# The last output group added onto x in its PSUM banks, and the last merged block turned later

## The chip, the core and the metric

The kernel runs on one core of a Trainium2 chip. The metric is the device time of one execution in microseconds; the profile's span runs from the first to the last instruction. The engines are TensorE (PE, with its weight loads PEld), VectorE (DVE), ScalarE (ACT), GpSimd (POOL) and SyncE (SP), which issues most of the DMAs.

## The reference

One decoder block over 256 tokens of width 2048: two token mixers, joined by sigmoid gates, an output projection, a residual and a final norm.

```python
xn = rmsnorm(x, norm_w)
rq, rk, rv, rz, dq, dk, dv, dz, g_ret, g_diff = split(xn @ w_in)
o_ret = rmsnorm(retention(rq, rk, rv)) * silu(rz)
o_diff = rmsnorm(diff_attention(dq, dk, dv, lam), subln_w) * (1 - lam_init) * silu(dz)
mixed = sigmoid(g_ret) * (o_ret @ w_ret_up) + sigmoid(g_diff) * (o_diff @ w_diff_up)
h = x + mixed @ w_out
out = rmsnorm(h, final_norm_w)
```

The change touches the last three lines: how the last quarter of `mixed` is laid out for the projection, the projection with `w_out`, the residual and the norm.

## The kernel before

**Units.** Every weight is read once, in units of 512 KB: 384 units in a row, through a ring of four buffers (`raw`, `w_hi`, `w_lo`). A unit is loaded by SyncE, rounded to `w_hi` by ScalarE (L711), its rest put into `w_lo` by VectorE (L1038), and multiplied by TensorE in three passes (hi by hi, hi by lo, lo by hi). The left side is split in the same way. ScalarE and VectorE split a unit three units ahead of TensorE (`AHEAD`), as soon as the unit four before it is done. The load of unit n waits on SyncE until unit n-4 is split. Every engine's queue is in order, and the Python loops fix what stands behind what: on SyncE a loop over n, on ScalarE and VectorE a loop over steps s, each of which first splits unit s+3 and then does its other work.

**The last two phases.** From `U_TAIL` on (units 320 to 351) `o_diff @ w_diff_up` is made in four groups j of 512 columns, eight units each. When a group is done, `merge_diff` multiplies it by the gate, `add_diff` adds it to `mixed`, `turn_mixed` transposes 32x32 squares into `squares_t` on VectorE, SyncE's `turn_mixed` moves the squares to their place in `rot` by 2 x 4 DMAs (L510), and `read_mt_hi` and `read_mt_lo` (L912, L1364) split the turned block into four k-tiles of `xt_hi` and `xt_lo`. From `U_OUT` on (units 352 to 383) `mixed @ w_out` is made in two groups of 1024 columns, 16 k-tiles each; tile k of the first is unit 352+k. TensorE holds `own` and `shared` banks, four each, and the two groups swap them. Tiles 4 and 5, and 10 and 11 (`SEVEN_AT`), are multiplied as a 2x2 block product in seven instead of eight products. That needs sums of token tiles (`sum_tokens`, split by `round_token_sums` and `rest_of_token_sums`) and sums of weight blocks (`sum_weights` L970 to L976, which stands in front of the split of the unit before them and waits until both units have landed; `round_sums` and `rest_of_sums` L990 split the sums). The seven products go to the own banks and, as parts, to the shared ones.

**The block and the group.** The last block (j = 3) gives k-tiles 12 to 15. It is merged in step 32, added and transposed in step 34, turned by SyncE in front of the load of unit 362 (tile 10), and read in step 38. TensorE waits for it (`ready`, count 8) in front of tile 12. x is loaded again for each block into `gate`, behind the loads of tiles 4 and 12 for the last two.

**The end of a group.** `copy_first` (ScalarE) and `join_shared` (VectorE, four instructions, L1019 to L1024) turn the parts into one summand for each of the four output tiles. `add_x` (L1374) adds x to them, `add_own` (L1382) adds the own bank. In the second group the last four tiles are multiplied bank by bank, 12 matmuls each, so that the banks end one after another. Row 0 is squared, normed and stored while row 1 is still being made. For row 1 the last tile is squared in two halves, on ScalarE (L923) and on VectorE (L1439), then come the sums (L1431), POOL's power (L662), and the scaling of the last two tiles on VectorE (L1446) and of the first two on ScalarE (L932).

## Time and profile before

| | |
|---|---|
| median of 3 runs | 1096.87 us (1094.86 to 1097.81) |
| the profiled execution | 1095.23 us |
| its span | 1093.4 us |
| TensorE busy | 1077.5 us, 99% |
| VectorE busy | 746.3 us, 68% |
| ScalarE busy | 540.5 us, 49% |
| mean granted TensorE clock | 0.995 |
| start of the first output group, last matmul | 992.3 us, 1083.2 us |

The engines overlap, so their busy times do not add up to the span. A matmul row shows 0.39 us of which about 0.23 us is its own turn, as the next starts then. The granted clock is a share of 2.4 GHz.

### The profile page before, as it was taken

What the parts mean: (1) busy time and instruction counts of PE and PEld (TensorE: products, weight loads), DVE (VectorE), ACT (ScalarE), POOL (GpSimd) and SP (SyncE); (2) the same over time, 40 slices, a digit from 0 to 9 for tenths busy, and PEclk for the clock granted to TensorE, in tenths of its full rate; (3) what the DMA queues carried; (4) which work ended last, traced back from release to release, by engine and by line L of the source; (5) the groups of instructions that cost most, each with busy time, mean ns of one, the idle gap of its engine ahead of it and who ended that gap; (6) DMA issues with size and microseconds to landing.
All of it is one profiled execution on the core that took longest, in us unless ns stands there. A gap on an engine that the chain in (4) does not pass through costs nothing.

```text
span 1093.4 us, 13197 instructions
## 1 busy us (share of the span) xinstructions
PE 1077.5 (99%) x4864; PEld 895.5 (82%) x4864; DVE 746.3 (68%) x919; ACT 540.5 (49%) x695; POOL 36.6 (3%) x57
## 2 busy tenths in 40 slices
PE   9999999999999999999999999999999999999996
PEld 7888888888888888888888888888888888887784
DVE  6685574585566688766856676676757674768796
ACT  6654455344555545444654465346544644445453
POOL 0100000000000000000100010000100020000000
PEclk9999999999999999999999999999999999999998
DMA  9887667776666565777576757676767667676653
GB/s 329 301 247 222 175 199 205 202 202 210 195 189 201 186 213 167 222 214 215 177 212 186 239 169 212 191 227 187 200 210 207 187 207 254 225 228 210 230 174 115
DMA packets 133985, 227.98 MB, mean 208 GB/s; under 512 B 14496, under 2 KB 40864, under 8 KB 133408
## 3 DMA queue, kind: packets, MB, share of 16 engines
q1 hardware_dynamic: 133632, 226.86, 67.9%
q8 instruction: 38, 0.62, 0.2%
q10 hardware_dynamic: 288, 0.27, 0.1%
q14 instruction: 27, 0.22, 0.1%
HBM read 210.84 MB, written 2.10 MB: 195 GB/s over the span
## 4 chain that ended last, share of the span: by engine, by line
PE 95%; DVE 2%; DMA 1%; ACT 1%; issue 1%; SPq 0%; DVEq 0%; POOLq 0%; POOL 0%; ACTq 0%
PE bank L1531 26%; PE bank L1529 26%; PE bank L1530 26%; PE bank L1536 4%; PE bank L1537 4%; PE bank L1538 4%; DMA raw<-w_out_dram 1%; PE bank L1599 1%; PE bank L1598 1%; PE bank L1597 1%; DVE w_lo L1038 1%; DMA raw<-w_in_dram 0%; PE bank L1712 0%; PE bank L1501 0%; ACT w_hi L711 0%
## 5 line engine op out<-in xcount | busy, mean ns | idle before, releaser
L1038 DVE TENSOR_TENSOR w_lo<-raw,w_hi 128x1024 fp32r<-128x1024 f32 x364 | 449.2, 1240 | 303.5 <-ACT w_hi L711 302.9
L711 ACT ACTIVATE w_hi<-raw 128x1024 fp32r<-128x1024 f32 x364 | 385.4, 1060 | 473.7 <-PE bank L1531 398.9
L1529 PE MATMUL bank<-w_hi,xt_hi 128*128 128x512 f32 x1136 | 443.3, 390 | 0.0
L1531 PE MATMUL bank<-w_hi,xt_lo 128*128 128x512 f32 x1136 | 442.1, 389 | 0.0
L1530 PE MATMUL bank<-w_lo,xt_hi 128*128 128x512 f32 x1136 | 442.0, 389 | 0.0
L1531 PEld LDWEIGHTS bank<-w_hi,xt_lo 128*128 128x128 f32 x1136 | 213.2, 188 | 44.5
L1530 PEld LDWEIGHTS bank<-w_lo,xt_hi 128*128 128x128 f32 x1136 | 213.3, 188 | 43.8
L1529 PEld LDWEIGHTS bank<-w_hi,xt_hi 128*128 128x128 f32 x1136 | 213.3, 188 | 43.8
L1529 PE MATMUL bank<-w_hi,ot_hi 128*128 128x512 f32 x128 | 49.8, 389 | 0.0
L1530 PE MATMUL bank<-w_lo,ot_hi 128*128 128x512 f32 x128 | 49.8, 389 | 0.0
L1531 PE MATMUL bank<-w_hi,ot_lo 128*128 128x512 f32 x128 | 49.8, 389 | 0.0
L1536 PE MATMUL bank<-w_hi,xt_hi 128*128 128x512 f32 x104 | 41.4, 399 | 3.6 <-DVE w_lo L1038 3.6
L1537 PE MATMUL bank<-w_lo,xt_hi 128*128 128x512 f32 x104 | 41.1, 396 | 0.0
L1538 PE MATMUL bank<-w_hi,xt_lo 128*128 128x512 f32 x104 | 41.0, 394 | 0.0
L1536 PE MATMUL bank<-w_hi,ot_hi 128*128 128x512 f32 x104 | 40.5, 389 | 0.0
L1537 PE MATMUL bank<-w_lo,ot_hi 128*128 128x512 f32 x104 | 40.5, 389 | 0.0
L1538 PE MATMUL bank<-w_hi,ot_lo 128*128 128x512 f32 x104 | 40.5, 389 | 0.0
L655 POOL TENSOR_TENSOR zs<-zs,sub 128x512 f32<-128x512 f32 x8 | 14.1, 1786 | 496.1 <-DVE zs L1105 496.1
L1530 PEld LDWEIGHTS bank<-w_lo,ot_hi 128*128 128x128 f32 x128 | 24.0, 188 | 5.0
L1531 PEld LDWEIGHTS bank<-w_hi,ot_lo 128*128 128x128 f32 x128 | 24.0, 188 | 5.0
L1529 PEld LDWEIGHTS bank<-w_hi,ot_hi 128*128 128x128 f32 x128 | 24.0, 188 | 4.9
L679 ACT ACTIVATE w_hi<-raw 128x1536 fp32r<-128x1536 f32 x8 | 11.9, 1491 | 31.8 <-PE bank L1538 24.7
(182 smaller groups left out, 851.8 us busy)
## 6 DMA issues: line engine op xcount, KB each, us to landing
raw<-w_in_dram SPq DMA_DIRECT2D x284, 512.0 KB, 4.3
raw<-w_ret_up_dram SPq DMA_DIRECT2D x32, 512.0 KB, 4.5
raw<-w_diff_up_dram SPq DMA_DIRECT2D x32, 512.0 KB, 4.8
raw<-w_out_dram SPq DMA_DIRECT2D x32, 512.0 KB, 4.6
rot<-squares_t SPq DMA_DIRECT2D x96, 64.0 KB, 2.4
zs<-squares_t SPq DMA_DIRECT2D x48, 64.0 KB, 2.2
normed<-squares_t SPq DMA_DIRECT2D x48, 64.0 KB, 2.2
raw<-w_in_dram SPq DMA_DIRECT2D x8, 256.0 KB, 4.8
```

Source lines behind the costliest of these rows:

```text
L655: pool.tensor_tensor(z, z, sub08[:, :].unsqueeze(1).broadcast_to([P, 2, V]), ALU.mult) \
L679: act.activation(hi_blocks[:, KU * s + 1:KU * s + 4, :], raw_blocks[:, KU * s + 1:KU * s + 4, :], ACT.Copy) \
L711: act.activation(w_hi[:, s, :, :], raw[:, s, :, :], ACT.Copy).then_inc(hi_ready, 1)
L1038: dve.tensor_tensor(w_lo[:, s, :, :], raw[:, s, :, :], w_hi[:, s, :, :].bitcast(F32), ALU.subtract) \
L1529: pe.matmul(bank[bk][:, :], hi, w_hi[:, s, kk, :], start=k == 0, stop=False)
L1530: pe.matmul(bank[bk][:, :], hi, w_lo[:, s, kk, :], start=False, stop=False)
L1531: return pe.matmul(bank[bk][:, :], lo, w_hi[:, s, kk, :], start=False, stop=k == KT - 1)
L1536: pe.matmul(dst, hi, w_hi_block, start=start, stop=False)
L1537: pe.matmul(dst, hi, w_lo_block, start=False, stop=False)
L1538: return pe.matmul(dst, lo, w_hi_block, start=False, stop=stop)
L1597: pe.matmul(dst, hi, v_hi[:, b, cols], start=start, stop=False)
L1598: pe.matmul(dst, hi, v_lo[:, b, cols], start=False, stop=False)
```

## The change

Five things change.

1. The last block is added in step 36, transposed in step 37, turned by SyncE in front of the load of unit 366 (tile 14) and read in step 41 (`tail_step`). The other blocks keep their places.
2. `sum_tokens` and the two functions behind it work on one pair of tiles at a time; for the output projection the first pair is summed in step 22, the second in step 29 (`TAIL_SUMS`). TensorE waits for each pair by itself.
3. The x loads of the last two blocks go behind the loads of tiles 17 and 18 (`X_AGAIN_AT`). `x_to_banks` copies x from `gate` into the four own banks of the second group, and TensorE's first products of this group add to it. `add_x` falls away for this group. The joined parts are added to the row-0 tiles in `add_own`, and to the row-1 tiles inside their banks (`part_to_bank`); TensorE waits for these before the last products of bank 2 and bank 3.
4. The row-1 tiles of the second group are squared by ScalarE (`square_last`) and scaled by VectorE (`scale_last`) straight from their banks; the halves and one scalar step go.
5. For the second pair of the second group the weight sums are split in front of the split of tile 12, not behind it (`sums_first`).

```diff
+TAIL_SUMS = (2 * UNITS + 6, 3 * UNITS + 5)
+X_AGAIN_AT = (U_TAIL + 20, U_TAIL + 28, U_OUT + 17, U_OUT + 18)
+def sums_first(n):
+    return n >= U_OUT + KT + KU * SEVEN_AT[-1]
-def merged_at(j):
-    return 1 if j < GROUPS_D - 1 else 2
-def merged_read_at(j):
-    return 4 if j < GROUPS_D - 1 else 6
+def tail_step(j, u, late):
+    return (j + 1) * UNITS + (late if j == GROUPS_D - 1 else u)
 # SyncE
-                        if j >= 0 and u_behind == merged_at(j):
+                    for j in range(GROUPS_D):
+                        if behind - U_TAIL == tail_step(j, 1, 6):
                             for b in range(BLOCKS):
                                 turn_mixed(j, b)
-                    if n > U_TAIL + 12 and (n - U_TAIL - 12) % UNITS == 0 and (n - U_TAIL - 12) // UNITS <= GROUPS_D:
+                    if n in X_AGAIN_AT:
 # ScalarE
+            def x_to_banks():
+                group = 2 * PAIR_GROUPS - 1
+                act.wait_ge(x_again[PAIR_GROUPS - 1], 16 * 2)
+                act.wait_ge(shared_drained, group)
+                for i in range(SUMS):
+                    b, j = pair_blocks(group)[i]
+                    act.activation(bank[pair_banks(group)[0][i]][:, :], gate[:, b, j * COLS:(j + 1) * COLS], ACT.Copy) \
+                       .then_inc(x_in_banks, 1)
+            def square_last(i):
+                e = SUMS + i
+                b, j = pair_blocks(PAIR_GROUPS - 1)[i]
+                own_full(act, 2 * PAIR_GROUPS - 1, i)
+                act.wait_ge(h_squared, e)
+                act.activation(junk[:, e % 2, :], bank[pair_banks(2 * PAIR_GROUPS - 1)[0][i]][:, :], ACT.Square,
+                               accum_out=h_ss[:, b, j:j + 1]).then_inc(h_squared, 1)
+                if out_s == KT - 2:
+                    x_to_banks()
             square_h(SUMS)
             square_h(SUMS + 1)
+            square_last(2)
             scale_h(0)
-            square_h(SUMS + 2)
-            square_h(SUMS + 3)
+            square_last(3)
             scale_h(1)
 # VectorE, split_lo (split_hi on ScalarE alike)
+                sums_behind = group is not None and k % KU == 0 and k // KU - 1 in SEVEN_AT
+                if sums_behind and sums_first(n):
+                    rest_of_sums(group, k // KU - 1)
                 dve.wait_ge(hi_ready, n + 1)
                 dve.tensor_tensor(w_lo[:, s, :, :], raw[:, s, :, :], w_hi[:, s, :, :].bitcast(F32), ALU.subtract) \
                    .then_inc(units_split, 2)
-                if group is not None and k % KU == 0 and k // KU - 1 in SEVEN_AT:
+                if sums_behind and not sums_first(n):
                     rest_of_sums(group, k // KU - 1)
 # VectorE, the tail loop
+                for j in range(GROUPS_D):
+                    if s == tail_step(j, 0, 0):
+                        merge_diff(j)
+                    if s == tail_step(j, 0, 4):
+                        add_diff(j)
+                    if s == tail_step(j, 1, 5):
+                        turn_mixed(j)
+                    if s == tail_step(j, 4, 9):
+                        read_mt_lo(j, 0)
+                        read_mt_lo(j, 1)
+            def part_to_bank(group, i):
+                dst = bank[pair_banks(group)[0][i]][:, :]
+                dve.wait_ge(shared_drained, group + 1)
+                dve.tensor_tensor(dst, dst, shared_part(group, i), ALU.add).then_inc(parts_in_banks, 1)
 # VectorE, the end
-            for i in range(SUMS):
-                add_x(group, i)
+            part_to_bank(group, 2)
+            part_to_bank(group, 3)
...
-            add_own(group, 2)
             dve.wait_ge(h_squared, SUMS + 3)
             add_square(1, j + 1, h_most, h_more, 1)
-            add_own(group, 3)
-            square_half()
-            dve.wait_ge(h_row_step[1], 2)
-            add_square(1, GROUPS_D, h_more, h_sum, 3)
             dve.wait_ge(h_squared, SUMS + 4)
-            add_square(1, j, h_sum, h_ms, 4)
-            dve.wait_ge(h_row_step[1], 5)
-            scale_h(1, j)
-            scale_h(1, j + 1)
+            add_square(1, j, h_more, h_ms, 2)
+            dve.wait_ge(h_row_step[1], 3)
+            own_full(dve, group, 3)
+            scale_last(3)
+            scale_last(2)
 # TensorE
+                    if onto_x(n) and i >= 2:
+                        pe.wait_ge(parts_in_banks, i - 1)
-                                 lo_blocks[:, block_at, :], k == 0, k == KT - 1)
+                                 lo_blocks[:, block_at, :], k == 0 and not onto_x(n), k == KT - 1, onto_x(n))
-                if group % PAIR_GROUPS:
+                if joined:
+                    pe.wait_ge(x_in_banks, SUMS)
+                elif group % PAIR_GROUPS:
```

`scale_last(i)` is the old scaling instruction with the bank as its input; `onto_x(n)` is true for the units of the second group.

## Rows read from the trace of the kernel before

**Rows 1.** The page, section 1: busy time of each engine.

```profile
PE 1077.5 (99%) x4864; PEld 895.5 (82%) x4864; DVE 746.3 (68%) x919; ACT 540.5 (49%) x695; POOL 36.6 (3%) x57
```

**Rows 2.** Waits of TensorE over the whole span: total, times, longest us.

```profile
PE bank L1536 <- DVE w_lo L1038: 3.6, 2, 2.5
```

**Rows 3.** Timeline of TensorE, first output group: start us, us, instruction, idle before it.

```profile
1006.60 0.50 PE L1536 MATMUL bank<-w_hi,xt_hi 128*128 128x512 f32 x1 [1.11 <-DVE w_lo L1038]
...
1020.30 0.50 PE L1536 MATMUL bank<-w_hi,xt_hi 128*128 128x512 f32 x1 [2.52 <-DVE w_lo L1038]
...
1026.79 0.39 PE L1536 MATMUL bank<-w_hi,xt_hi 128*128 128x512 f32 x1
```

**Rows 4.** Two stretches of the first output group: busy us, clock, DMA.

```profile
1020.30:1024.70 4.40, 4.40 (x12) 3.50 (x13) 4.40 (x5) 0.76 (x1) 0.00 (x0) 0.61 0.45 154
1024.70:1034.00 9.30, 9.30 (x42) 7.69 (x41) 6.68 (x6) 4.73 (x5) 0.00 (x0) 1.00 0.91 300
```

**Rows 5.** Timeline of TensorE, second output group.

```profile
1069.63 0.50 PE L1536 MATMUL bank<-v_hi,xt_hi 128*128 128x512 f32 x1 [0.52 <-DVE v_lo L990]
...
1083.16 0.39 PE L1538 MATMUL bank<-w_hi,xt_lo 128*128 128x512 f32 x1
```

**Rows 6.** Timeline of VectorE, the end of the kernel.

```profile
1075.45 0.68 DVE L1024 TENSOR_TENSOR rot<-rot,bank 128x512 f32<-128x512 f32 x1
...
1085.41 0.69 DVE L1382 TENSOR_TENSOR gate<-gate,bank 128x512 f32<-128x512 f32 x1
...
1086.85 0.21 DVE L1431 TENSOR_SCALAR h_ms<-h_ss,h_sum 128x1 f32<-128x1 f32 x1
1087.79 1.42 DVE L1446 SCALAR_TENSOR_TENSOR mixed<-gate,h_rstd,zs 128x512 f32<-128x512 f32 x2 [0.73 <-POOL h_rstd L662]
```

**Rows 7.** Timeline of ScalarE, the end of the kernel.

```profile
1084.40 0.63 ACT L923 ACTIVATE junk<-gate 128x512 bf16<-128x512 f32 x1 [0.73 <-DVE gate L1382]
```

**Rows 8.** Timeline of VectorE, first output group.

```profile
987.45 1.22 DVE L994 TENSOR_TENSOR probs<-xt_hi,xt_lo 128x1024 f32<-128x1024 f32 x1
...
996.34 1.23 DVE L970 TENSOR_TENSOR mixed<-raw 128x1024 f32<-128x1024 f32 x1 [1.57 <-DMA raw<-w_out_dram]
...
1001.27 1.75 DVE L984 TENSOR_TENSOR w_lo<-raw,w_hi 128x1536 fp32r<-128x1536 f32 x1
1002.94 1.29 DVE L1351 TENSOR_TENSOR mixed<-mixed,gate 128x512 f32<-128x512 f32 x2
...
1005.36 1.19 DVE L1038 TENSOR_TENSOR w_lo<-raw,w_hi 128x1024 fp32r<-128x1024 f32 x1
1006.47 2.28 DVE L990 TENSOR_TENSOR v_lo<-mixed,v_hi 128x2048 fp32r<-128x2048 f32 x1
...
1016.43 1.23 DVE L970 TENSOR_TENSOR mixed<-raw 128x1024 f32<-128x1024 f32 x1 [5.41 <-DMA raw<-w_out_dram]
...
1019.02 1.22 DVE L1038 TENSOR_TENSOR w_lo<-raw,w_hi 128x1024 fp32r<-128x1024 f32 x1
1020.16 1.29 DVE L1364 TENSOR_TENSOR xt_lo<-rot,xt_hi 128x512 fp32r<-128x512 f32 x2
```

**Rows 9.** The chain that ended last, between 1000 and 1024 us.

```profile
1010.72 5.61 DMA raw<-w_out_dram
```

**Rows 10.** Timeline of SyncE's queue, first output group.

```profile
1004.92 5.12 SPq L510 DMA_DIRECT2D rot<-squares_t  x8
```

**Rows 11.** Timeline of ScalarE, first output group.

```profile
1003.46 1.06 ACT L711 ACTIVATE w_hi<-raw 128x1024 fp32r<-128x1024 f32 x1
...
1011.67 1.15 ACT L912 ACTIVATE xt_hi<-rot 128x512 fp32r<-128x512 f32 x2 [1.49 <-DMA rot<-squares_t]
```

**Rows 12.** Weight loads (L499, 990 to 1012 us): issue in ns, us to landing.

```profile
L499 SPq DMA_DIRECT2D raw<-w_out_dram x8: 327/379/589, 991.4 to 1011.2; - x8
...
DMA to landing us min/median/max: 3.2/4.9/6.4
```

**Rows 13.** The four x loads (L579) of the whole span: us to landing.

```profile
DMA to landing us min/median/max: 6.6/6.9/7.2
```

More of the change, by code:

```diff
@@ L457, in build @@
         final_w = zs[:, :, :].rearrange("p b n -> p (b n)")
-        def seven_tiles(t):
-            first, step = KU * SEVEN_AT[0], KU * (SEVEN_AT[1] - SEVEN_AT[0])
-            return t[:, first:first + N_SEVEN * step, :].rearrange("p (a x) t -> p a x t", x=step)[:, :, 0:KU, :]
         def own_full(eng, group, i):
@@ L856, in _ @@
                     if it == RET_ITS - 1 and s == 60:
-                        round_token_sums(0)
+                        for a in range(N_SEVEN):
+                            round_token_sums(0, a)
             act.wait_ge(lam_step, 1)
@@ L990, in rest_of_sums, with sum_tokens @@
                 dve.tensor_tensor(v_lo[:, :, :], weight_sums(group)[:, :, :], v_hi[:, :, :].bitcast(F32), ALU.subtract).then_inc(sum_lo_ready, 1)
-            def sum_tokens(phase, hi, lo):
-                dve.tensor_tensor(whole, seven_tiles(hi).bitcast(F32), seven_tiles(lo).bitcast(F32), ALU.add) \
+            def sum_tokens(phase, a, hi, lo):
+                count, tiles = N_SEVEN * phase + a, slice(KU * SEVEN_AT[a], KU * (SEVEN_AT[a] + 1))
+                dve.tensor_tensor(whole[:, a, :, :], hi[:, tiles, :].bitcast(F32), lo[:, tiles, :].bitcast(F32), ALU.add) \
@@ L995, in sum_tokens @@
                    .then_inc(reads_joined, 1)
-                dve.wait_ge(reads_joined, phase + 1)
-                a11, a12 = whole[:, :, 0, 0:P], whole[:, :, 1, 0:P]
-                a21, a22 = whole[:, :, 0, P:2 * P], whole[:, :, 1, P:2 * P]
-                dve.scalar_tensor_tensor(out=xsum[:, :, 0, :], in0=a21, scalar=-1.0, in1=a22, op0=ALU.mult, op1=ALU.subtract) \
+                dve.wait_ge(reads_joined, count + 1)
+                a11, a12 = whole[:, a, 0, 0:P], whole[:, a, 1, 0:P]
+                a21, a22 = whole[:, a, 0, P:2 * P], whole[:, a, 1, P:2 * P]
@@ L1000, in sum_tokens @@
+                dve.scalar_tensor_tensor(out=xsum[:, a, 0, :], in0=a21, scalar=-1.0, in1=a22, op0=ALU.mult, op1=ALU.subtract) \
                    .then_inc(sums_step, 1)
-                dve.tensor_tensor(xsum[:, :, 2, :], a11, a21, ALU.subtract)
-                dve.wait_ge(sums_step, 2 * phase + 1)
-                dve.scalar_tensor_tensor(out=xsum[:, :, 1, :], in0=xsum[:, :, 0, :], scalar=-1.0, in1=a11,
+                dve.tensor_tensor(xsum[:, a, 2, :], a11, a21, ALU.subtract)
+                dve.wait_ge(sums_step, 2 * count + 1)
@@ L1004, in sum_tokens @@
+                dve.scalar_tensor_tensor(out=xsum[:, a, 1, :], in0=xsum[:, a, 0, :], scalar=-1.0, in1=a11,
                                          op0=ALU.mult, op1=ALU.subtract).then_inc(sums_step, 1)
-                dve.wait_ge(sums_step, 2 * phase + 2)
-                dve.tensor_tensor(xsum[:, :, 3, :], a12, xsum[:, :, 1, :], ALU.subtract).then_inc(sums_ready, 1)
-            def rest_of_token_sums(phase):
-                dve.wait_ge(sums_hi_ready, phase + 1)
-                dve.tensor_tensor(xsum_lo, xsum, xsum_hi.bitcast(F32), ALU.subtract).then_inc(sums_lo_ready, 1)
+                dve.wait_ge(sums_step, 2 * count + 2)
@@ L1036, in split_lo @@
                     return
+                sums_behind = group is not None and k % KU == 0 and k // KU - 1 in SEVEN_AT
+                if sums_behind and sums_first(n):
+                    rest_of_sums(group, k // KU - 1)
                 dve.wait_ge(hi_ready, n + 1)
@@ L1039, in split_lo @@
                    .then_inc(units_split, 2)
-                if group is not None and k % KU == 0 and k // KU - 1 in SEVEN_AT:
+                if sums_behind and not sums_first(n):
                     rest_of_sums(group, k // KU - 1)
@@ L1220, in _ @@
                         dve.wait_ge(ot_lo_ready, SEVEN_AT[-1] + 1)
-                        sum_tokens(0, ot_hi, ot_lo)
+                        for a in range(N_SEVEN):
+                            sum_tokens(0, a, ot_hi, ot_lo)
                     if it == RET_ITS - 1 and s == 60:
-                        rest_of_token_sums(0)
+                        for a in range(N_SEVEN):
+                            rest_of_token_sums(0, a)
             dve.wait_ge(lambda_landed, 16 * 4)
@@ L1417, in _ @@
                     for i in range(SUMS):
[L1418 removed]
+                        add_x(i)
                 if out_s == KT - 2:
@@ L1433, in add_square, with scale_last @@
                 dve.wait_ge(h_row_step[b], step)
-            def square_half():
-                last = gate[:, 1, j * COLS + HALF:(j + 1) * COLS]
-                dve.wait_ge(h_ready, 2 * SUMS)
-                dve.tensor_tensor_reduce(out=squares_t[:, 0, 0:HALF], in0=last, in1=last, scale=1.0, scalar=0.0,
-                                         op0=ALU.mult, op1=ALU.add, accum_out=h_ss[:, 1, GROUPS_D:GROUPS_D + 1]) \
-                   .then_inc(h_row_step[1], 1)
+            def scale_last(i):
+                cols = slice(pair_blocks(group)[i][1] * COLS, (pair_blocks(group)[i][1] + 1) * COLS)
+                dve.scalar_tensor_tensor(out=mixed[:, 1, cols], in0=bank[pair_banks(group)[0][i]][:, :], scalar=h_rstd[:, 1:2],
+                                         in1=final_w[:, cols], op0=ALU.mult, op1=ALU.mult).then_inc(y_late, 1)
             def scale_h(b, c):
```

102 lines of the change are left out of this document (52 added, 50 removed).

## The prediction, made before the changed kernel had run

> **What bounds the kernel now.** I read the page first: TensorE is busy for 99% of the span [rows 1], so only two things can move the time: idle time of TensorE, and what stands before its first and behind its last matmul. The waits of TensorE come next. They name one real pair, 3.6 us in two waits for the low half of a weight unit [rows 2]. The timeline of TensorE puts them into the first output group: 1.11 us in front of tile 6 (1006.60) and 2.52 us in front of tile 9 (1020.30), both released by VectorE's split at L1038 [rows 3]. The second has an echo: its 12 matmuls took 4.40 us at a granted clock of 0.61, while the 42 behind them took 9.30 us, 0.221 each, at 1.00 [rows 4]. Half of a 2.4 GHz clock in part of that stretch cost 4.40 - 12 x 0.221 = 1.7 us. A last small idle of 0.52 us lies in the second output group, at 1069.63, for the low half of the weight sums (L990). After the last matmul at 1083.16 [rows 5] the kernel still needs ten microseconds, on VectorE, ScalarE and POOL [rows 6, 7].
>
> Why was VectorE late? In front of tile 6's split (1005.36) it did the addition and the transpose of the last merged block, from 1002.94: 2.42 us. Tile 9's split (1019.02) waited behind the sums of the weights of tiles 10 and 11, which waited for tile 11's load until 1016.43 [rows 8]. That load left at 1010.72 and took 5.61 us [rows 9]. It left so late because SyncE had first issued the eight transfers that turn the last block, 5.12 us from 1004.92 [rows 10].
>
> **Part 1: the last block is turned later.** Removed in front of tile 6: 2.42 us on VectorE. The split of tile 6 can start at 1002.94 instead of 1005.36 and TensorE's wait of 1.11 us (1.3 with its restart) goes. The halved token sums ahead of the group (five instructions, the first 1.22 us at 987.45, replaced by half widths, the other half done a block earlier) let tile 1's split, and so tile 5's load, start up to 1.1 us sooner. The sum at 996.34 waited for that load, so VectorE may be ahead by 0 to 1.1 us from there on. The low half of the weight sums needs the high half, which ScalarE finishes when it turns to tile 7 at 1003.46 [rows 11], so it can start at 1003.5 to 4.1 rather than 1006.47; 2.2 us later tile 7's split starts, and it ends 1.1 us after that, at 1006.9 to 1007.4.
>
> Tile 11's load now waits for that split alone. Weight loads landed in 3.2 to 6.4 us, median 4.9 [rows 12]; with tiles 8 and 9 released when the split of tiles 4 and 5 ended, at 1003.0 [rows 8], I take 4.5, so it lands at about 1011.6, 4.8 us sooner than before. The sums and tile 9's split take 1020.16 - 1016.43 = 3.73 us [rows 8]: split of tile 9 done at 1015.3. TensorE, without its waits, starts tile 6 at 1005.3 and tile 12 after 1026.79 - 1006.60 - 2.7 (wait) - 1.7 (clock) = 15.8 us, at 1021.1; tile 9 begins 4.8 us before that, at 1016.3. So the second wait and its clock loss go as well, by 1 us.
>
> But the turn is not gone. SyncE now issues it in front of tile 14's load, behind tile 13's, and tile 13's load waits for the split of tile 9. So the eight transfers start at 1015.3 + 0.4 (one load issued [rows 12]), take 5.1 us as in [rows 10], and end at 1020.8. ScalarE read the block 1011.67 - 1010.04 = 1.63 us after the last issue ended [rows 10, 11]; its two copies take 1.15 us, and the second subtraction of VectorE some 0.7 (two took 1.29 [rows 8]). The last tiles of the block are ready at 1020.8 + 1.6 + 1.15 + 0.7 = 1024.3, and TensorE's wait for all eight halves stands in front of tile 12, where it arrives at 1021.1. I expect a new wait of 3.2 us there, between 2 and 4.5. Queued behind it on TensorE are the weight-sum products, tile 13 and the rest of the group; ScalarE's and VectorE's splits of tile 13 stand behind their reads of the block, but are not needed for 5 us. An idle of 2.52 us was followed by the slow stretch of 1.7 us, one of 1.11 us was not [rows 3, 4]; the new idle is longer than both, so I take 1.7 again (bounds 0 and 3.4, none and two such stretches).
>
> Sum of part 1: tile 12 starts at 1024.3 instead of 1026.8, 2.5 us sooner; less the clock, 1.7: 0.8 us gained, where the two waits and the clock looked like 5.7.
>
> The rule that speaks on this: the Trainium skill, "DMA: Bandwidth & Descriptors", section "Issuing engines are not separate DMA queues", says that a sequencer's time to start a DMA is usually small against the DMA itself. The trace disagrees here: eight issues took 5.12 us and the landing came 1.6 us after them. By the rule the turn would be over 5 us sooner, no wait would be left in front of tile 12, and the kernel would gain 5.7 us instead of 0.8 in this part.
>
> **Part 2: x goes into the banks.** Added on ScalarE: four copies 128x512 into banks 0 to 3 in step 14 of the first output group. The trace has no ScalarE write into PSUM; the nearest is its square of a 128x512 tile at 0.63 us [rows 7], and bounds of 0.5 and 1.0 each give 2 to 4 us. They wait for the joined parts of the group, which before were done in time for the same start of the second group, and for two x loads that now go out behind tiles 17 and 18. Those took 6.6 to 7.2 us [rows 13]. Tile 18's load waits for tile 14's split, which I put at 1028; x lands near 1036, the copies end near 1039, and TensorE reaches the second group near 1040.4, 60 matmuls behind 1026.8 (60 took 13.5 us from 1069.63 to 1083.16 [rows 5]; after the change the same within 1 us). Cover of 1.5 us, so it costs nothing; without it each late us is a us. VectorE loses the four additions of x in the second group. The token sums of the earlier output phase are cut in two as well, five more short instructions on VectorE and one on ScalarE; I price them at nothing, since TensorE waits for neither engine there [rows 2], and at 1 us if that cover were thin.
>
> **Part 3: sums ahead of the split in the second group.** v_lo no longer stands behind tile 12's split (1.1 us). The idle of 0.52 us goes, with its restart 0.6 us. Tile 15, whose split ends where the join begins (three additions of 0.7 before 1075.45 [rows 6], so 1073.4), is then needed nine matmuls into the last products, at 1073.7: just in time. Gain 0.6, bounds 0.3 and 0.7.
>
> **Part 4: the end.** The joined parts are complete at 1075.45 + 0.68 = 1076.1 [rows 6]. Two additions inside banks take 0.7 each by the same row; the first ends at 1076.9, and TensorE, 0.6 us sooner than before, wants that bank half way through its last 48 matmuls of 10.9 us, at 1077.1. Cover of 0.2 us: if the write into PSUM costs more (bound 1.0 us), TensorE waits 0.1 us. After the last matmul (1083.16 - 0.6 = 1082.5) the old way was: addition, squares in two halves, two scalar steps, POOL, scaling at 1087.79, and VectorE was late for it too, beginning the addition at 1085.41, as it had still to scale the other rows [rows 6]. The new way: matmul complete after 0.4, square from the bank 0.63 and 0.15 for its sum [rows 7], then scalar step, POOL and hand-over in 1087.79 - 1086.85 = 0.94 [rows 6]: scaling starts at 1084.7. Stores follow as before. So the scaling is 3.1 us sooner, part 3 in it; bounds 2.3 and 3.4 (slower reads of PSUM in the square and in the scaling against none).
>
> **Sum.** 0.8 + 3.1 = 3.9 us. The profiled execution took 1095.23 us for a span of 1093.4: span 1089.5, time 1091.3. The median of the runs is 1.64 us above the profiled one, so I forecast 1096.87 - 3.9 = 1093.0 us.
>
> **Rivals.** *No wait at tile 12.* The turn is ready in time: its issues cost SyncE little, or SyncE is ahead. For it: nothing else on SyncE's queue is late. Against it: the chain from tile 7's split to the block is 17 us of rows, and TensorE needs 14. It would give 3.1 + 5.7 = 8.8 us, 1088.1. (The rule of the Trainium skill above leads to this case.) *The end gives less than it takes in the middle.* The slow stretch doubles to 3.4 us, or the additions inside the banks hold TensorE: part 1 turns to -0.9 and 2 to 2.3 us of gain are left, 1094.7. For it: the new idle is longer than any in the trace behind the start. *Slower: the turn comes still later.* Each us that tile 11's load is late moves tile 12 by one. To lose the whole gain the load has to take 4.5 + 3.9 = 8.4 us; above that the kernel is slower. The slowest weight load took 6.4, the slowest x load 7.2 [rows 12, 13]. At 12 us it is 3.6 us slower, 1100.5; less than that is enough if the slow stretch doubles too.
>
> **How the numbers follow.** Forecast 0.60, no wait at tile 12 0.10, middle takes more 0.23, slower 0.07. 0.3% of the median, about what a measurement of this kernel tells from no change, is 3.3 us; the forecast's own 3.9 lies close above it, so some 0.1 of its share falls below and half a tenth of the third case above. Of the slower case 0.05 lies beyond 0.3%. Faster 0.60, same 0.35, slower 0.05. The range holds the forecast with the bounds of its load, its clock and its end (gain 1 to 7) and the third case: 1089.2 to 1096.5; left out are most of the no-wait case and the slower one. The forecast's own range is 1091.5 to 1095.
>
> **What the profile of the changed kernel would show.** Right: no idle of TensorE in front of tiles 6 and 9; one idle of 2 to 4.5 us in front of tile 12, released by VectorE's read of the block (L1364 of before), with a slow clock behind it; the turn's eight issues behind a load at about 1015.7; no wait at the start of the second group; last matmul 0 to 2 us sooner than 1083.2 and 2.2 us between it and the last scaling. Wrong: the issues at 1010 or before and no idle at tile 12; an idle at the first tile of the second group; an idle between banks in its last products; a load of tile 11 over 6 us.

## The result and the profile after

| | before | after |
|---|---|---|
| median | 1096.87 us | 1091.02 us (5 runs, 1089.04 to 1092.02) |
| the profiled execution | 1095.23 us | 1090.99 us |
| its span | 1093.4 us | 1089.1 us |
| last matmul | 1083.16 us | 1080.99 us |
| last scaling begins (VectorE) | 1087.79 us | 1083.51 us |

The ratio of the times is 0.9949, with a 95% interval of 0.9939 to 0.9960: faster by half a per cent. The forecast was 1093.0 us in a range of 1089.2 to 1096.5. The medians differ by 5.85 us, the two profiled executions by 4.24, and my sum was 3.9. Two more executions of the kernel before took 1095.53 us and, far outside all others, 1554.62 us; with both its median is still 1096.87.

The page of the changed kernel, busy times, beside [rows 1]:

```profile
PE 1077.8 (99%) x4864; PEld 897.1 (82%) x4864; DVE 744.9 (68%) x924; ACT 543.0 (50%) x701; POOL 36.4 (3%) x57
```

TensorE has the same work in a span that is 4.3 us shorter. The waits of TensorE, beside [rows 2]: two waits for the low half of a weight unit have become one for the low half of the turned block.

```profile
PE bank L1572 <- DVE xt_lo L1396: 2.5, 1, 2.5
```

The timeline of TensorE shows where it lies. There is no idle in front of tiles 6 and 9 any more [rows 3]. Tile 12 is the row at 1023.70:

```profile
1020.85 0.39 PE L1574 MATMUL bank<-w_hi,xt_lo 128*128 128x512 f32 x1
1023.70 0.78 PE L1572 MATMUL bank<-w_hi,xt_hi 128*128 128x512 f32 x1 [2.47 <-DVE xt_lo L1396]
...
1026.42 0.63 PE L1572 MATMUL bank<-w_hi,xt_hi 128*128 128x512 f32 x1
1026.84 0.55 PE L1573 MATMUL bank<-w_lo,xt_hi 128*128 128x512 f32 x1
1027.23 0.39 PE L1574 MATMUL bank<-w_hi,xt_lo 128*128 128x512 f32 x1
```

Behind the idle the matmuls start 0.43 us apart, the 1.2 GHz level, until 1027.23, where they go back to 0.23. From 1020.85 to 1027.23 nine starts took 6.38 us instead of 9 x 0.227 = 2.04, so this place costs 4.3 us. The windows of the same stretches (columns as in [rows 4]; the seventh is the granted clock) say it in another way:

```profile
992.50:1020.90 28.40, 28.40 (x127) 23.48 (x125) 23.87 (x24) 12.86 (x10) 0.00 (x0) 1.00 0.56 181
1023.70:1027.70 4.00, 4.00 (x11) 3.20 (x12) 2.70 (x3) 2.21 (x3) 0.00 (x0) 0.57 0.99 365
1027.70:1038.60 10.90, 10.90 (x50) 9.03 (x49) 8.87 (x12) 4.77 (x7) 0.00 (x0) 1.00 0.67 252
```

How the block comes to be late is read from SyncE's queue and from ScalarE and VectorE (timelines, beside [rows 8, 10, 11]):

```profile
1014.96 5.08 SPq L511 DMA_DIRECT2D rot<-squares_t  x8
```

```profile
1021.69 1.15 ACT L916 ACTIVATE xt_hi<-rot 128x512 fp32r<-128x512 f32 x2 [2.31 <-DMA rot<-squares_t]
...
1034.74 2.14 ACT L936 ACTIVATE bank<-gate 128x512 f32<-128x512 f32 x4
```

```profile
1010.70 1.23 DVE L995 TENSOR_TENSOR mixed<-raw 128x1024 f32<-128x1024 f32 x1
...
1013.29 1.22 DVE L1068 TENSOR_TENSOR w_lo<-raw,w_hi 128x1024 fp32r<-128x1024 f32 x1
...
1019.42 2.29 DVE L1015 TENSOR_TENSOR v_lo<-mixed,v_hi 128x2048 fp32r<-128x2048 f32 x1 [0.51 <-ACT v_hi L688]
1022.35 1.29 DVE L1396 TENSOR_TENSOR xt_lo<-rot,xt_hi 128x512 fp32r<-128x512 f32 x2 [0.65 <-ACT xt_hi L916]
```

VectorE takes up tile 11 at 1010.70 without a wait, where before it stood 5.41 us for it. Tile 9's split ends at 1014.5, SyncE issues the eight transfers behind it, the block has landed 1.65 us after the last issue, and the second read ends at 1023.64. The row at 1034.74 is x going into four banks, 0.54 us each; it waits for no transfer.

The end, VectorE first and then ScalarE, beside [rows 6, 7]:

```profile
1074.17 0.68 DVE L1051 TENSOR_TENSOR rot<-rot,bank 128x512 f32<-128x512 f32 x1
1074.88 1.30 DVE L1425 TENSOR_TENSOR bank<-bank,squares_t 128x512 f32<-128x512 f32 x2
...
1082.21 0.21 DVE L1473 TENSOR_SCALAR h_ms<-h_ss,h_more 128x1 f32<-128x1 f32 x1 [0.88 <-ACT junk L945]
1083.51 1.41 DVE L1480 SCALAR_TENSOR_TENSOR mixed<-bank,h_rstd,zs 128x512 f32<-128x512 f32 x2 [1.08 <-POOL h_rstd L662]
```

```profile
1081.42 0.60 ACT L945 ACTIVATE junk<-bank 128x512 bf16<-128x512 f32 x1 [0.30 <-PE bank L1574]
...
1083.15 1.33 ACT L954 ACTIVATE mixed<-mixed,h_rstd 128x512 f32<-128x512 f32 x2 [1.04 <-POOL h_rstd L662]
```

ScalarE's last square now waits for TensorE. The scaling on VectorE begins 2.52 us after the last matmul, where it was 4.63. So the scaling is 4.28 us sooner: 2.17 from an earlier last matmul and 2.11 behind it.

### The profile page after: what moved, and what is told of

Read it like the earlier page. It is cut to its first block, busy times and chain, and to the rows that moved or that the text cites. A ratio compares the mean times of both kernels' runs of the same rounds, so it can differ in the third digit from the quotient of the medians.

```text
span 1089.1 us, 13206 instructions
## 1 busy us (share of the span) xinstructions
PE 1077.8 (99%) x4864; PEld 897.1 (82%) x4864; DVE 744.9 (68%) x924; ACT 543.0 (50%) x701; POOL 36.4 (3%) x57
## 4 chain that ended last, share of the span: by engine, by line
PE 95%; DVE 2%; issue 1%; DMA 1%; ACT 1%; SPq 0%; DVEq 0%; POOL 0%; POOLq 0%; ACTq 0%
PE bank L1565 26%; PE bank L1567 26%; PE bank L1566 26%; PE bank L1572 4%; PE bank L1573 4%; PE bank L1574 4%; PE bank L1642 1%; PE bank L1641 1%; PE bank L1640 1%; DVE w_lo L1068 0%; DMA raw<-w_out_dram 0%; PE bank L1537 0%; SPq L511 0%; PE bank L1541 0%; PE bank L1520 0%
```

## The experiments

Two questions were open: which of the five changes earns what, and why the medians moved 2 us more than my sum. "Idle at 12" is TensorE's wait in front of tile 12; "lost" is what all starts of matmuls more than 0.26 us apart, from 992 us on, cost above 0.227 each. It holds the idles, the slow stretches and the restarts: behind an idle the second matmul starts 0.33 us after the first, not 0.23.

| run | median | ratio to before (95%) | idle at 12, us | lost, us | last matmul | last scaling |
|---|---|---|---|---|---|---|
| before | 1096.87 | | 0 | 6.57 | 1083.16 | 1087.79 |
| changed | 1091.02 | 0.9949 (0.9939 to 0.9960) | 2.47 | 4.38 | 1080.99 | 1083.51 |
| e1_late_only | 1096.59 | 1.0001 (0.9992 to 1.0009) | 3.33 | 7.39 | 1084.19 | 1089.67 |
| e2_all_but_late | 1092.39 | 0.9962 (0.9950 to 0.9974) | 0 | 6.32 | 1083.08 | 1085.59 |
| e3_turn_one_load_sooner | 1089.17 | 0.9934 (0.9922 to 0.9946) | 1.73 | 2.36 | 1079.30 | 1081.83 |
| e4_half_turn_on_act | 1088.56 | 0.9931 (0.9919 to 0.9943) | 1.73 | 2.00 | 1078.66 | 1081.17 |
| e5_sums_behind | 1091.67 | 0.9958 (0.9946 to 0.9970) | 2.68 | 3.74 | 1080.70 | 1083.21 |
| e6_end_through_gate | 1094.18 | 0.9976 (0.9967 to 0.9985) | 3.5 | 5.70 | 1082.65 | 1086.84 |
| e7_before_again | 1097.33, one run | | 0 | 7.47 | 1084.46 | 1089.90 |
| e8_read_before_sums | 1088.35 | 0.9925 (0.9913 to 0.9937) | 0 | 0.90 | 1078.01 | 1080.52 |
| e9_x_sooner | 1088.22 | 0.9926 (0.9913 to 0.9938) | 0 | 1.28 | 1078.01 | 1080.53 |
| e10_changed_again | 1091.03 | 0.9949 (0.9936 to 0.9961) | 2.78 | 4.63 | 1081.32 | 1083.85 |
| e11_end_through_gate_again | 1093.98 | 0.9975 (0.9965 to 0.9986) | 3.32 | 5.45 | 1082.10 | 1086.28 |
| e12_bank_by_bank | 1089.49 | 0.9936 (0.9922 to 0.9949) | 0 | 2.96 | 1079.77 | 1082.32 |

The kernel before had medians of 1096.3 to 1096.7 us beside these runs.

### e1, e2: the late turn alone, and all the rest alone

e1 is the kernel before with change 1 alone; e2 is the changed kernel with the block at its old places.

```diff
# e1, on the kernel before (SyncE; VectorE and ScalarE alike)
-                        if j >= 0 and u_behind == merged_at(j):
+                        if behind - U_TAIL == tail_step(j, 1, 6):
# e2, on the changed kernel
-tail_step(j, 1, 6), tail_step(j, 0, 4), tail_step(j, 1, 5), tail_step(j, 4, 9)
+tail_step(j, 1, 2), tail_step(j, 0, 2), tail_step(j, 1, 2), tail_step(j, 4, 6)
```

> The kernel before with only the late places of the last block (added in step 36, transposed in 37, turned in front of tile 14's load, read in step 41). Theory (the gain of the late turn is mostly given back in front of tile 12): no idle in front of tiles 6 and 9, one idle of 2.5 to 3.5 us in front of tile 12 with a slow clock of some 1.6 us behind it, span 1.0 to 2.0 us under the kernel before, ratio 0.998 to 0.999. Rival (the late turn brings the 5.7 us that its two waits and clock cost): idle under 1 us, ratio 0.995. Rival (the token sums in two halves are what makes VectorE early): an idle of 1 us or more in front of tile 9 stays.

> The changed kernel with the last block back at its old places; x in the banks, halved token sums, sums in front of the split and the new end stay. Theory: 2.1 us from the end and 0.7 from the sums of the second group, so 2.8 us under the kernel before, ratio 0.9975; both old idles in the first group (1.1 and 2.5 us) with the slow clock are back, the second perhaps 0.5 us shorter, as the x load behind tile 12's load is gone. Rival (the x loads and the halved sums remove the waits of the first group): idles under 1 us in sum there, ratio 0.993.

The late turn alone gains nothing (1.0001), where I expected 1 to 2 us, and the rest alone gains 4.2 us, where I expected 2.8. The idles came where I expected them in both; e1's slow stretch was longer, 2.8 us against 1.6. TensorE in e1, timeline:

```profile
1024.61 0.79 PE L1529 MATMUL bank<-w_hi,xt_hi 128*128 128x512 f32 x1 [3.33 <-DVE xt_lo L1359]
```

The two old idles are gone and this one has come, with 0.43 us between matmuls until 1030.67: 6.36 us lost at one place, where the old two with their slow stretch lost 5.8 in the profile of [rows 3, 4] and 6.4 in e7. VectorE's timeline of e1 shows why the idle is longer than in the changed kernel: here it still waited for tile 11's load.

```profile
1011.61 1.23 DVE L965 TENSOR_TENSOR mixed<-raw 128x1024 f32<-128x1024 f32 x1 [0.79 <-DMA raw<-w_out_dram]
```

The sum began 0.91 us later than in the changed kernel, the turn (1015.88) 0.92 us later, tile 12 0.91 us later. In e2 the old idles are back:

```profile
1006.23 0.50 PE L1572 MATMUL bank<-w_hi,xt_hi 128*128 128x512 f32 x1 [0.62 <-DVE w_lo L1068]
...
1019.84 0.50 PE L1572 MATMUL bank<-w_hi,xt_hi 128*128 128x512 f32 x1 [2.42 <-DVE w_lo L1068]
```

e2 also waits twice for the splits of tiles 14 and 15 of the second group (0.29 and 0.34 us), as their loads came late there. Behind the last matmul it has the new 2.51 us. So the late turn is worth nothing alone and some 1.4 us on top of the rest (1092.39 against 1091.02; the intervals of the two ratios overlap, so the size is uncertain).

### e3, e4: is it SyncE's issuing that holds the block?

e3 issues the turn one load sooner, behind the load that waits for tile 8's split. e4 keeps the place on SyncE and gives four of the eight transfers to ScalarE's queue, where they also go out 4 us sooner.

```diff
# e3
-                        if behind - U_TAIL == tail_step(j, 1, 6):
+                        if behind - U_TAIL == tail_step(j, 1, 5):
# e4, SyncE
-                            for b in range(BLOCKS):
+                            for b in range(BLOCKS if j < GROUPS_D - 1 else 1):
# e4, ScalarE, step GROUPS_D * UNITS + 6
+                    act.wait_ge(squares_ready[1], tail_turns(GROUPS_D - 1) + 1)
+                    for i in range(STRIPS):
+                        act.dma_start(rot[:, 1, ...], squares_t[..., 1, ...])
```

> The changed kernel with the eight issues of the turn in front of tile 13's load instead of tile 14's; nothing else moves. Theory (the block is late because SyncE waits for tile 9's split before it issues the turn): issues begin at 1010.8 instead of 1015.0, the block is ready at 1019.5, no idle in front of tile 12, no slow clock: 2.6 + 1.6 = 4.2 us under the changed kernel, span 1084.9, ratio to the kernel before 0.991. Rival (the turn's transfers are slow because of the weight loads in flight, not because of their place): the idle shrinks by less than 2 us. Rival (tile 13's load, now 5 us later, makes TensorE wait in front of tile 13): a new idle of 1 us or more there.

> The changed kernel, where ScalarE issues the four transfers of the second row block in step 38 and SyncE only the other four, at the late place. Theory (SyncE's time to issue, 0.64 us each, is on the path): SyncE is done with the turn 2.5 us sooner, idle in front of tile 12 is 0.0 to 0.5 us, no slow clock, 3.9 us under the changed kernel, ratio to the kernel before 0.991 to 0.992. Rival (issue time is small beside the transfers): idle stays above 2 us, ratio 0.995. ScalarE pays 2.5 us in a stretch in which it was idle for 4.7.

e3 gained 1.9 us over the changed kernel and e4 2.5, and in both the idle shrank only to 1.73 us; the expectation that it would go was wrong. No slow stretch followed it in either, and no new idle came in front of tile 13. The two queues of e4, timelines:

```profile
1015.13 2.49 SPq L511 DMA_DIRECT2D rot<-squares_t  x4
```

```profile
1010.84 2.65 ACTq L964 DMA_DIRECT2D rot<-squares_t  x4
```

What stopped them is in the timeline of VectorE in e3:

```profile
1019.63 2.29 DVE L1015 TENSOR_TENSOR v_lo<-mixed,v_hi 128x2048 fp32r<-128x2048 f32 x1 [0.51 <-ACT v_hi L688]
1021.84 1.29 DVE L1396 TENSOR_TENSOR xt_lo<-rot,xt_hi 128x512 fp32r<-128x512 f32 x2
```

There is no wait in front of the read at 1021.84: the block was there, and VectorE was at the low half of the weight sums, which TensorE needs later than the block. ScalarE was at the high half of these sums in the same way, and so were both engines in e4. In the changed kernel VectorE stood only 0.65 us in front of this read (the row at 1022.35 above). So the issues held the block by no more than that, and the rest of the gain is the slow stretch that did not follow. VectorE's own order was the next bound, 0.5 us behind.

### e8, e9, e12: the waits behind it

e8 takes e3 and puts the read of the last block in front of the weight sums, on both engines. e9 also loads x two units sooner. e12 also lets TensorE wait for each bank of x by itself, and turns round two waits in front of the last scaling.

```diff
# e8, in split_lo behind the split of tile 12 (split_hi alike, with read_mt_hi), over e3
+                if n == U_OUT + 12:
+                    read_mt_lo(GROUPS_D - 1, 0)
+                    read_mt_lo(GROUPS_D - 1, 1)
...
-                    if s == tail_step(j, 4, 9):
+                    if j < GROUPS_D - 1 and s == tail_step(j, 4, 9):
# e9
-X_AGAIN_AT = (U_TAIL + 20, U_TAIL + 28, U_OUT + 17, U_OUT + 18)
+X_AGAIN_AT = (U_TAIL + 20, U_TAIL + 28, U_OUT + 15, U_OUT + 16)
# e12, TensorE and VectorE
-                    pe.wait_ge(x_in_banks, SUMS)
+                if onto_x(n) and k == 0:
+                    pe.wait_ge(x_in_banks, i + 1)
...
-            dve.wait_ge(h_row_step[1], 3)
             own_full(dve, group, 3)
+            dve.wait_ge(h_row_step[1], 3)
```

> The turn in front of tile 13's load, and both engines split the turned block between tile 12's split and the weight sums, not behind the sums. Theory (with the turn sooner the rest of the idle, 1.7 us, is VectorE's 2.2 us for the low half of the weight sums, which stands in front of the block's): the block is ready at 1020.3, TensorE does not wait in front of tile 12, nor 2.7 us later for the sums; 2.0 us under the kernel with the turn sooner alone, ratio to the kernel before 0.9915 to 0.992. Rival (the sums then wait): an idle of 1 us or more between tile 12 and the products of the weight sums.

> The kernel of the run before (turn in front of tile 13's load, block split before the weight sums), with the two x loads behind the loads of tiles 15 and 16 instead of 17 and 18. Theory (ScalarE waited 2.7 us for x, and with it TensorE 0.9 us at the start of the second group, a wait that the changed kernel hides behind its idle in front of tile 12): x lands 5 us sooner, no idle there, 0.7 to 1.1 us under that kernel, ratio to the kernel before 0.9915 to 0.992. Rival (ScalarE's copies, 2.2 us, or the joined parts hold the start): the idle stays above 0.5 us.

> The kernel of e9 (turn sooner, block before the sums, x loads behind tiles 15 and 16) with two small edits that the profile can tell apart. One: TensorE waits for the copies of x bank by bank (one copy before each bank's first product) instead of for all four. Theory: the 0.77 us lost at the start of the second group shrink to 0.2 or less, as the copies take 0.54 each and the products of a bank 0.68. Two: VectorE waits for the last product before it waits for the norm, not behind it. Theory (a wait between the norm and the scaling costs the 0.36 us by which VectorE starts later than ScalarE): 1.30 us from the last scalar step to the scaling become 0.94. Rival (reading a bank costs it): 1.30 stays. In sum 0.5 to 1.1 us under e9, ratio to the kernel before 0.992.

In e8 the first group runs without any idle, as expected, and the second begins with one. Of the 2.0 us that I expected under e3 the median shows 0.8. TensorE and ScalarE in e8, timelines:

```profile
1035.95 0.47 PE L1578 MATMUL bank<-w_hi,xt_hi 128*128 128x512 f32 x1 [0.65 <-issue]
```

```profile
1033.69 2.16 ACT L939 ACTIVATE bank<-gate 128x512 f32<-128x512 f32 x4 [2.73 <-DMA gate<-x_dram]
```

ScalarE's copies waited for x and ended at 1035.85, and TensorE began 0.1 us later: the cover that the prediction gave them (part 2) is gone once the group comes 3 us sooner. In e9 x is there, and the same instruction waits for the last join of VectorE instead:

```profile
1033.13 2.16 ACT L939 ACTIVATE bank<-gate 128x512 f32<-128x512 f32 x4 [1.53 <-DVE rot L1054]
```

It starts only 0.56 us sooner, and 0.13 us of lost time is won at this place, while 0.52 us is lost in front of 1044.08, where TensorE waits for a weight split. The two versions have the same time; the 0.7 to 1.1 us that I expected did not come. In e12 the idle at the start of the group is gone and comes back 8 us later, larger, as the timelines of TensorE and VectorE show:

```profile
1042.81 0.39 PE L1580 MATMUL bank<-w_hi,xt_lo 128*128 128x512 f32 x1
1044.50 0.50 PE L1578 MATMUL bank<-w_hi,xt_hi 128*128 128x512 f32 x1 [1.30 <-DVE w_lo L1071]
```

```profile
1037.11 1.88 DVE L1425 TENSOR_TENSOR gate<-gate,bank 128x512 f32<-128x512 f32 x3
1038.90 1.22 DVE L1071 TENSOR_TENSOR w_lo<-raw,w_hi 128x1024 fp32r<-128x1024 f32 x1
1040.04 0.68 DVE L1425 TENSOR_TENSOR gate<-gate,bank 128x512 f32<-128x512 f32 x1
1040.64 1.22 DVE L998 TENSOR_TENSOR mixed<-raw 128x1024 f32<-128x1024 f32 x1
...
1043.23 1.22 DVE L1071 TENSOR_TENSOR w_lo<-raw,w_hi 128x1024 fp32r<-128x1024 f32 x1
```

VectorE goes without a pause from the join to that split; it is the bound there, and a TensorE that starts sooner only waits longer. e12 lost a further 1.3 us at the splits of tiles 14 and 15, whose loads came late. Its median is 1.3 us above e9's, with overlapping intervals, where I expected 0.5 to 1.1 us less: the expectation missed. e8 and e9, at 1088.35 and 1088.22 us, beat both the kernel before (by 0.7%) and the changed kernel.

### e5: the weight sums behind the split again

```diff
-    return n >= U_OUT + KT + KU * SEVEN_AT[-1]
+    return False
```

> The changed kernel with the weight sums of the second group's second pair split behind tile 12's split again, as before the change. Theory (the sums in front give the 0.5 us idle back and no more): an idle of 0.5 us with its restart in front of those products, 0.5 to 0.8 us over the changed kernel, ratio to the kernel before 0.995 to 0.996. Rival (TensorE then only waits later, for tiles 14 and 15): the same time as the changed kernel within 0.2 us, the idle moved.

The old idle is back in TensorE's timeline, as in [rows 5], and costs 0.80 us with its restart:

```profile
1067.18 0.50 PE L1572 MATMUL bank<-v_hi,xt_hi 128*128 128x512 f32 x1 [0.53 <-DVE v_lo L1015]
```

The median is 0.65 us above the changed kernel's, as expected, but the intervals of the two ratios overlap: the row shows the price better than the median does. Its profile has no slow stretch behind 2.68 us of idle at tile 12.

### e6, e11: the last tiles through SBUF

The joined parts still go into the banks, but the last two tiles are copied to `gate` by VectorE, and squared and scaled from there.

```diff
-            square_last(2)
             scale_h(0)
-            square_last(3)
+            square_h(SUMS + 2)
+            square_h(SUMS + 3)
             scale_h(1)
# VectorE, and the same for tile 3
+            own_full(dve, group, 2)
+            dve.tensor_copy(gate[:, b, jj * COLS:(jj + 1) * COLS], bank[pair_banks(group)[0][2]][:, :])
...
-            scale_last(3)
-            scale_last(2)
+            scale_h(1, j)
+            scale_h(1, j + 1)
```

> The changed kernel, but VectorE copies the two row-1 tiles of the second group from their banks to SBUF (0.68 us each, in the place of the old additions) and ScalarE squares and VectorE scales them from there. Theory (the end is shorter because VectorE's pass over the last tile is off the path and it no longer stands behind the scaling of row 0): 1.6 to 2.0 us between the last matmul and the last scaling come back (2.5 to 4.3), ratio to the kernel before 0.996 to 0.997. Rival (the gain of the end comes from the second group's start and from earlier row-0 norms): under 0.8 us.

> The kernel whose row-1 tiles go through SBUF at the end, once more, beside the changed kernel on the same chip. Theory: 1.7 us over the changed kernel, the 1.67 us between last matmul and last scaling that its profile showed; the 3.2 us of the first timing held some 1.5 us of a longer idle in front of tile 12. Rival (the copies cost TensorE time too): 2.5 us or more again, with new waits of TensorE in its last products.

Both were some 3.0 us slower than the changed kernel, where I expected some 1.7. VectorE in e11, timeline:

```profile
1075.17 0.68 DVE L1051 TENSOR_TENSOR rot<-rot,bank 128x512 f32<-128x512 f32 x1
...
1080.81 1.42 DVE L1486 SCALAR_TENSOR_TENSOR mixed<-gate,h_rstd,zs 128x512 f32<-128x512 f32 x2 [0.74 <-POOL h_rstd L662]
1082.14 0.68 DVE L1510 COPY gate<-bank 128x512 f32<-128x512 f32 x1
1083.61 0.21 DVE L1473 TENSOR_SCALAR h_more<-h_ss,h_most 128x1 f32<-128x1 f32 x1 [0.79 <-ACT junk L926]
1083.86 0.69 DVE L1510 COPY gate<-bank 128x512 f32<-128x512 f32 x1
...
1086.28 1.41 DVE L1486 SCALAR_TENSOR_TENSOR mixed<-gate,h_rstd,zs 128x512 f32<-128x512 f32 x2 [0.72 <-POOL h_rstd L662]
```

Neither copy has an idle in front of it that ends with TensorE. From VectorE's last join addition on, the end is a chain of VectorE, ScalarE's squares and POOL's power, and nothing in it waits for TensorE: 1086.28 - 1075.17 = 11.11 us here and 11.10 in e6. The kernel before has 1087.79 - 1075.45 = 12.34 [rows 6], e7 12.35 and e1 12.35, while the changed kernel has 9.34 (9.65 in e10) and ends by TensorE: its last square waits for the last matmul. The end through SBUF so costs some 1.7 us: 4.18 us from the last matmul to the scaling, where the changed kernel has 2.52. The rest, 1.1 us in e11 and 1.7 in e6, lies ahead of the last matmul: the idle at tile 12 was 3.3 to 3.5 us in both runs. The traces show how it came. The first sums of the group waited for their load until 996.75 in both, against 995.51 in the changed kernel and 995.90 in e10. Tile 11's load left at 1007.9 and VectorE had it at 1011.81 and 1012.07, and the turn was issued at 1016.08 and 1016.33, 1.1 and 1.4 us later than in the changed kernel. All this lies far ahead of the code that was edited. Why an edit of the end makes the loads late I did not find.

### e7, e10: both kernels again

> The kernel before, unchanged, for one more profile. Its profiled execution was 1.6 us under the median of its runs, that of the changed kernel was at its median. Theory (the slow clock behind the second idle lasts longer in most executions): span 1094 to 1096, the idles as before (1.1, 2.5), but more than the 1.6 us lost to the slow clock. Rival (executions differ all along the span): the same 1.6 us there, the difference in front of 992 us.

> The changed kernel, unchanged, beside the others on one chip. Theory: ratio to the kernel before 0.995 within 0.001; the idle in front of tile 12 2.3 to 3.5 us, the slow clock behind it between nothing and 3 us in different executions. Rival (its first timing was a lucky one): ratio 0.997.

The changed kernel came out the same to 0.01 us in its median. Its profile again had one idle, 2.78 us, and a slow stretch of 1.58 us behind it. The kernel before had longer waits than in the profile that I had read, but its slow stretch was not longer, as I had expected it to be: eight starts 0.43 us apart, behind an idle of 3.15 us. Waits of TensorE in e7, beside [rows 2]:

```profile
PE bank L1536 <- DVE w_lo L1038: 4.3, 2, 3.1
```

It lost 7.47 us in all, where the profile of [rows 3 to 5] lost 6.57 counted in the same way, and had 5.44 us between the last matmul and the scaling, where that had 4.63 (e1, with the same end, has 5.48). ScalarE shows where the 0.8 us at the end come from. In front of tile 14's rounding it waited 2.59 us for the load in e7 and 1.69 in the profile before; the splits, and with them the join additions, came later by about as much. Timelines of ScalarE, the profile before first, then e7:

```profile
1069.89 2.14 ACT L711 ACTIVATE w_hi<-raw 128x1024 fp32r<-128x1024 f32 x2 [1.69 <-DMA raw<-w_out_dram]
```

```profile
1072.07 2.01 ACT L711 ACTIVATE w_hi<-raw 128x1024 fp32r<-128x1024 f32 x2 [2.59 <-DMA raw<-w_out_dram]
```

The old end hangs on the last loads in this way; the new one ends by TensorE.

## Why the prediction was right, and where it was off

**The late turn trades two waits for one: right.** No idle at tiles 6 and 9, one at tile 12 of 2.47 us (I said 3.2, between 2 and 4.5), released by the read of the block, with a slow stretch of 1.6 us (I said 1.7). That the stretch came is partly luck: I took it because the idle would be longer than 2.52 us, and e5 has none behind 2.68 us. The steps of the sum held one by one:

| | predicted | measured |
|---|---|---|
| VectorE takes up tile 11 | 1011.6 | 1010.70, no wait |
| tile 9's split ends | 1015.3 | 1014.5 |
| the turn is issued | 1015.7 | 1014.96 |
| its last issue ends | 1020.8 | 1020.04 |
| the block is read | 1024.3 | 1023.64 |
| TensorE arrives at tile 12 | 1021.1 | 1021.1 |

The whole chain is 0.7 us or more sooner, because the load of tile 11 was: I took 4.5 us for it, and in e10, e5, e11, e6 and e1, where VectorE waits for it, it took 3.69, 3.60, 3.79, 4.05 and 4.23. So the losses of the first group fell by 1.4 us (5.8 to 4.3) and not by 0.8. e1 says that the late turn alone is worth nothing; the rest, 3.1 in my sum, made 4.2 by itself in e2.

**The rule on issuing: the trace speaks against it, but it would not have removed the wait.** Eight issues took 5.08 us, and the wait at tile 12 shrank both when they came one load sooner (e3) and when SyncE issued half of them (e4). The Trainium skill, "DMA: Bandwidth & Descriptors", section "Issuing engines are not separate DMA queues", calls such time usually small against the transfer; the measurement decides against it here. One issue was 0.64 us where its transfer landed 2.2 us after it (median of the eight), and the eight issues stand one behind another in the queue. My reading that issues of no length would leave no wait at tile 12 was wrong as well: with the block there in time e3 and e4 still waited 1.73 us, for VectorE's order.

**x into the banks costs nothing: right, but the cover is 2 us thick.** The copies took 0.54 us each and ended at 1036.9. TensorE reached the second group at about 1038.9: 1080.99 less the 42.1 us that lie between the group's start and its last matmul in e8, where an idle marks the start. e8 took the cover away and showed the idle.

**Sums ahead of the split: right.** 0.6 predicted, with bounds of 0.3 and 0.7; e5 gave 0.65 in the median and 0.80 of lost time in the trace. "Tile 15 just in time" held too: no wait in the changed kernel, only one start 0.04 us late at 1072.60, behind the end of tile 15's split; but 0.3 us for each of tiles 14 and 15 in e2, 0.23 in e6 for one of them, 0.48 and 0.27 in e12.

**The additions inside the banks: right.** The two took 1.30 us together, as two additions in SBUF do [rows 8], and TensorE, which may not start the last products of these two banks before them, went on starting matmuls 0.23 us apart.

**The end: mis-sized twice.** I had 2.2 us from the last matmul to the scaling; it is 2.52. VectorE's scaling from a bank began 0.36 us after ScalarE's, where in [rows 6] the two, both from SBUF, begin together. The larger fault is what I took the old end to be. "After the last matmul the old way was: ..." counts from TensorE, though I had seen that VectorE was late for it. VectorE was not a little late. The chain that begins with its last join addition was the bound: 12.35 us to the scaling in three traces, wherever the last matmul stood (4.63, 5.44 and 5.48 us ahead of the scaling). Against that chain the new end saves 12.34 - 9.34 = 3.0 us by the changed kernel's profile and 2.7 by e10's, where I had 2.4.

**The sum against the profiled execution was close, 3.9 against 4.24, and partly by luck. The step to the median failed.** Up to the last matmul I had 1.4 us (0.8 and 0.6) and 2.17 came; behind it I had 2.4 and 2.11 came. The two errors have opposite signs. The median itself, 1091.02 us, lies just outside the forecast's own range of 1091.5 to 1095. I added the 1.64 us by which the runs lay above the profiled execution to both kernels. It belongs to the old one: the changed kernel's profiled executions are 0.03 us below its median and, in e10, 0.24 above. Measured against e7, an execution of the kernel before that lies 0.5 to 1.0 us above its medians, the changed kernel gains 1084.46 - 1080.99 = 3.47 us before the last matmul and 5.44 - 2.52 = 2.92 behind it, 6.39 together, and the two times differ by 1097.33 - 1090.99 = 6.34. So, as far as two profiles of the kernel before tell, most of the surplus lies in what the change removes, and what was shorter in the one execution I read: of the 2.1 us between e7 and that execution 0.6 are in the idle in front of tile 9 (3.15 against 2.52) and 0.8 in the end. That these differ from one execution to the next, and that both follow a load that came later, is measured; what makes the loads come at different times isn't.

**The rivals.** No wait at tile 12 was given 1088.1 us. It was not what the changed kernel does, but e8 builds it, by another place of the turn and of the read, and has 1088.35. The middle gave more than was forecast, 1.4 us against 0.8, and not less; e1, with 3.33 us of idle and a slow stretch of 2.8, is what that rival looks like. The slower case did not come either: tile 11's load was there before VectorE asked for it.

**Open.** Why the loads ahead of tile 12 come later in e6 and e11, and why those of tiles 14 and 15 come late in e2, e6 and e12. No run takes out the halved token sums or the copies of x by themselves, so what each of these two earns or costs isn't shown. Why 1.4 us is gained where the late turn meets the rest is partly shown: tile 11's load was 0.9 us sooner for VectorE than in e1, and the waits of e2 at tiles 14 and 15 are not there.

## What to carry to other kernels

When an idle is removed from an engine that is 99% busy, work out when each other engine reaches the next hand-over: here the limit went from tile 9 to SyncE's issues, then to VectorE's order, to the load of x, to VectorE's queue, each within a microsecond or two of the one before. Count a tail from the last step behind which nothing waits for the busy engine, not from the last matmul: here that was VectorE's last join addition. And a wait read from one profile is one draw: where the median lies above the profiled execution, the difference may belong to the very waits that the change removes, so profile the kernel before twice.

## What the runs showed of the hardware

- The slow stretch behind an idle of TensorE is not fixed by the length of the idle: none behind 1.73 us (e3, e4) and 2.68 us (e5); eight starts of matmuls some 0.43 us apart behind 2.47 us (the changed kernel), 2.52 (before), 2.78 (e10), 3.15 (e7) and 3.32 (e11); thirteen behind 3.33 us (e1), but six behind 3.53 us (e6).
- ScalarE wrote 128x512 from SBUF into a bank in 0.54 us, where its squares of the same shape took 0.63 us from SBUF and 0.60 us from a bank. Two VectorE additions with one input and the output in a bank took 1.30 us together, as two in SBUF did (1.29).
- VectorE's scaling that reads a bank began 0.35 to 0.39 us after ScalarE's, though both wait for the same POOL result; that from `gate` begins with ScalarE's (e11: 1086.28 for both). e12 turned the two waits in front of it round, and 0.39 us stayed, so their order isn't the cause. Whether it is the read of the bank or that there is a second wait, no run tells apart.
- Issuing on SyncE cost 0.64 us for each of the eight small transfers of the turn, 0.33 to 0.59 us (median 0.38, [rows 12]) for a weight load of 512 KB and 0.43 us for a load of x.
